# Tuned two-block fp32 kernel on one core: second tiles awaited at use, rotations behind a third tile, one input loaded later, half of the cross output begun inside the attention, roots by exp(-ln/2), squares summed last

## The reference

```python
for i in range(DEPTH):                      # first block, two layers
    u = rms_norm(h, g_mix_norm[i])
    h = h + token_mixers(u, w_in[i], ...)   # two attentions, gates, w_branch_a/b, w_out
    h = h + conv_ffn(rms_norm(h, g_ffn_norm[i]), w_up[i], conv_w[i], conv_b[i], w_down[i])
    ple_gate = jax.nn.sigmoid(rms_norm(h, g_ple_norm[i]) @ w_ple_gate[i])
    h = h + ple_gate * (p[i] @ w_ple_proj[i])
for i in range(DEPTH):                      # second block, two layers
    # mixer of four groups (convolutions, a recurrence, an attention) @ w_out, added to h
    # q = rms_norm(rms_norm(h) @ x_wq, x_qn), k likewise of mem; o = attention(q, k, v) @ x_wo, added
    # h = h + (silu(n @ w1) * (n @ w3)) @ w2   with n = rms_norm(h)
```

## Time and profile before

| | |
|---|---|
| three runs | 3471.82, 3479.12, 3483.51 us; median 3479.12 |
| profiled execution, own time | 3473.41 us |
| its span | 3471.6 us |
| TensorE busy | 3182.2 us, 92% of the span |
| VectorE, ScalarE, GpSimd busy | 1679.7 (48%), 1434.4 (41%), 1576.5 us (45%) |
| mean granted TensorE clock | 0.951 |
| HBM read | 260.46 MB, 76 GB/s over the span |

### The profile page before, as it was taken

The page is one execution under the profiler, slowest core; times in us unless marked ns, Lnnn a source line. Parts: engine busy times, 40 slices in busy tenths (PEclk is TensorE's granted clock), DMA queues, the critical chain, the costliest instruction groups (busy, mean ns, idle before and its releaser), DMA issues. The chain is left out here.

```text
span 3471.6 us, 39165 instructions
## 1 busy us (share of the span) xinstructions
PE 3182.2 (92%) x14620; PEld 2475.1 (71%) x14620; DVE 1679.7 (48%) x2524; ACT 1434.4 (41%) x2281; POOL 1576.5 (45%) x870
## 2 busy tenths in 40 slices
PE   7978999999998799999999968899999985979999
PEld 6655688878776567887878736578877862758887
DVE  2673347731358533775245884433313785443320
ACT  4826533333384564333343444432223354352221
POOL 4623545544564355554555332344445432234443
PEclk8989999999899999999999978999999997889999
DMA  3211233333221122333322101123333200213333
GB/s 113 61 55 42 68 93 97 97 97 103 76 61 61 35 62 93 98 97 95 108 82 90 50 12 44 61 85 97 98 96 98 68 25 20 72 48 98 96 98 103
DMA packets 73740, 265.09 MB, mean 76 GB/s; under 512 B 8656, under 2 KB 9168, under 8 KB 73168
## 3 DMA queue, kind: packets, MB, share of 16 engines
q1 hardware_dynamic: 73552, 262.59, 24.6%
HBM read 260.46 MB, written 2.10 MB: 76 GB/s over the span
## 5 line engine op out<-in xcount | busy, mean ns | idle before, releaser
L365 POOL TENSOR_TENSOR low<-raw,high 128x1024 fp32r<-128x1024 f32 x482 | 1171.1, 2432 | 1289.2 <-ACT high L356 1269.3
L380 PE MATMUL bank<-slot_r,low 128*128 128x512 f32 (+2 forms) x3636 | 1434.5, 395 | 0.0
L381 PE MATMUL bank<-slot_r,high 128*128 128x512 f32 (+2 forms) x3636 | 1431.9, 394 | 0.0
L379 PE MATMUL bank<-slot_r,high 128*128 128x512 f32 (+1 forms) x3316 | 1337.6, 403 | 75.0 <-POOL low L365 30.8
L356 ACT ACTIVATE high<-raw 128x1024 fp32r<-128x1024 f32 x482 | 506.7, 1054 | 821.3 <-PE bank L381 761.0
L379 PEld LDWEIGHTS bank<-slot_r,high 128*128 128x128 f32 x3316 | 635.0, 192 | 260.1 <-issue 69.6
L380 PEld LDWEIGHTS bank<-slot_r,low 128*128 128x128 f32 (+1 forms) x3636 | 696.6, 192 | 149.0 <-issue 9.4
L381 PEld LDWEIGHTS bank<-slot_r,high 128*128 128x128 f32 (+1 forms) x3636 | 695.5, 191 | 149.4
L1583 DVE SCALAR_TENSOR_TENSOR tmp<-padded,small,tmp 128x512 f32<-128x512 f32 x176 | 210.0, 1251 | 0.0
L840 POOL TENSOR_SCALAR tmp<-tmp,stat 128x512 f32<-128x512 f32 (+3 forms) x128 | 71.5, 559 | 193.0 <-DVE stat L815 169.2
L509 ACT ACTIVATE slot_r<-slots,small 128x512 fp32r<-128x512 f32 (+1 forms) x80 | 54.7, 683 | 207.8 <-DVE slots L1591 73.4
(11 more groups left out here) (310 smaller groups left out, 3584.1 us busy)
## 6 DMA issues: line engine op xcount, KB each, us to landing
raw<-w SPq DMA_DIRECT2D x482, 512.0 KB, 3.6
slots<-x_in SPq DMA_DIRECT2D x4, 512.0 KB, 6.6
slots<-mem_in SPq DMA_DIRECT2D x2, 1024.0 KB, 5.0
out<-slots SPq DMA_DIRECT2D x8, 256.0 KB, 4.8
const<-const_in SPq DMA_DIRECT2D x1, 1073.5 KB, 10.8
padded<-p_in SPq DMA_DIRECT2D x2, 512.0 KB, 5.5
tmp<-masks_in SPq DMA_DIRECT2D x1, 512.0 KB, 11.5
small<-small SPq DMA_DIRECT2D x2, 231.5 KB, 2.7
```

Source lines behind the costliest of these rows:

```text
L365: pool.tensor_tensor(self.low[:, t % PARTS, :], self.raw[:, t % RING, :], self.high[:, t % PARTS, :].bitcast(F32), ALU.subtract).then_inc( ...
L379: pe.matmul(acc, lhs[0], rhs[1], start=first, stop=False)
L380: pe.matmul(acc, lhs[1], rhs[0], start=False, stop=False)
L381: return pe.matmul(acc, lhs[0], rhs[0], start=False, stop=last)
```

## The change

What it does, part by part. In `lead_tiles`, at w_out and the mix of `first_tail`, and at w_out and the query tiles of `second_tail`, the second of two tiles is awaited when its first product comes, not together with the first. In `first_project` the first two rotations stand behind the third tile. The transfer of `p` stands two weight tiles later. The second half of w_ple_proj waits for each bank by itself. In `second_tail` the roots are exp(-ln/2) on ScalarE and the three reciprocals are gone; the second value tile is split ahead of the query's roots; the first x_wo tile is split inside the attention and its four products with the first half of XO stand ahead of the last values; `hf` has seven buffers for squares, its low parts stand one step later, its adds behind all of them, and its total behind the second up tile.

```diff
@@ Prep @@
-        if c >= 3:
-            act.wait_ge(self.sig("added"), c - 2)
-        out = self.squares[c % 2] if c else self.acc
+        if c > len(self.squares):
+            act.wait_ge(self.sig("added"), c - len(self.squares))
+        out = self.squares[c % len(self.squares)] if c else self.acc
@@ lead_tiles; the same edit at mix and w_out of first_tail, at w_out and query of second_tail @@
-        two = [weights.next(pe) for _ in range(2)]
+        two = []
         for ks in (range(KC - 1), range(KC - 1, KC)):
-            for j, w in enumerate(two):
+            for j in range(2):
+                if len(two) == j:
+                    two.append(weights.next(pe))
+                w = two[j]
@@ first_project @@
-                    if j >= 1:
-                        rotate(j - 1)
+                    for n in ((), (), (0, 1))[j] if j < 3 else (j - 1,):
+                        rotate(n)
@@ first_tail @@
-                weights.load(sp, ffn + 2 * FC + 6)
+                weights.load(sp, ffn + 2 * FC + 8)
                 sp.wait_ge(sem("conv"), 6 * FC)
                 sp.dma_start(padded_t[:, 0:2, 0:SEQ], p_in[layer]).then_inc(sem("load_p"), 16)
...
-                    if half:
-                        pe.wait_ge(sem("ple_product"), 4)
                     w = weights.next(pe)
                     for c in range(4):
+                        if half:
+                            pe.wait_ge(sem("ple_product"), c + 1)
@@ second_tail @@
-        hf = Prep(sem, "hf", xs, [s2("g_ffn", c) for c in range(KC)], u_all, tmp[:, 4, :], [tmp[:, 5, :], tmp[:, 2, :]])
+        hf = Prep(sem, "hf", xs, [s2("g_ffn", c) for c in range(KC)], u_all, tmp[:, 4, :], [tmp[:, i, :] for i in (5, 2, 0, 1, 3, 8, 9)])
+        def side_pe(pe, step, place):
+            if step == 4 * NT + 4 and place == "turns":
+                out_tile.append(weights.next(pe))
+                pe.wait_ge(sem("o_low"), 1)
+                for n in range(4):
+                    product(pe, banks[n][:, :], part(out_tile[0], slice(None), slice(2 * n * P, 2 * n * P + P)), pair(XO_HIGH, XO_LOW), True, False)
+
+        def side_act(act, step):
+            if step == 2 * NT + 6:
+                act.wait_ge(sem("out_ready"), 2)
+                act.activation(R[XO_HIGH][:, :], S[:, XO, :], ACT.Copy).then_inc(sem("o_high"), 1)
+                weights.split_high(act, o_at + 1)
+
+        def side_dve(dve, step, place):
+            if step == 4 * NT and place == "end":
+                dve.wait_ge(sem("o_high"), 1)
+                dve.tensor_tensor(R[XO_LOW][:, :], S[:, XO, :], R[XO_HIGH][:, :].bitcast(F32), ALU.subtract).then_inc(sem("o_low"), 1)
+
+        def side_pool(pool, n):
+            if n == 2 * NT + 4:
+                weights.split_low(pool, o_at + 1)
...
-                    if s == 0:
+                    if s == 1:
                         hf.total(pe, banks[6][:, :], cst("ones"))
...
-                        act.activation(K_R, K_R, ACT.Sqrt, scale=1.0 / 64).then_inc(sem("key_root"), 1)
+                        act.activation(K_R, K_R, ACT.Ln, scale=1.0 / 64).then_inc(sem("key_log"), 1)
+                        act.wait_ge(sem("key_log"), 1)
+                        act.activation(K_R, K_R, ACT.Exp, scale=-0.5).then_inc(sem("key_rstd"), 1)
...
+                weights.split_high(act, q_at + 4)
                 for c in range(2):
                     act.wait_ge(sem("query_biased"), c + 1)
-                    act.activation(tmp[:, 2 + c, :], tmp[:, 2 + c, :], ACT.Sqrt, scale=1.0 / 64).then_inc(sem("query_root"), 1)
+                    act.activation(tmp[:, 2 + c, :], tmp[:, 2 + c, :], ACT.Ln, scale=1.0 / 64).then_inc(sem("query_log"), 1)
+                for c in range(2):
+                    act.wait_ge(sem("query_log"), c + 1)
+                    act.activation(tmp[:, 2 + c, :], tmp[:, 2 + c, :], ACT.Exp, scale=-0.5).then_inc(sem("query_rstd"), 1)
                 weights.split_high(act, q_at + 5)
...
-                        dve.wait_ge(sem("key_root"), 1)
-                        dve.reciprocal(K_R, K_R).then_inc(sem("key_rstd"), 1)
...
-                    dve.wait_ge(sem("query_root"), c + 1)
-                    dve.reciprocal(r, r).then_inc(sem("query_rstd"), 1)
...
                     dve.tensor_tensor(S[:, X + c, :], S[:, X + c, :], banks[c][:, :], ALU.add).then_inc(sem("x_crossed"), 1)
-                    hf.low(dve, c)
                     if c >= 1:
-                        hf.add(dve, c)
+                        hf.low(dve, c - 1)
+                hf.low(dve, KC - 1)
+                for c in range(1, KC):
+                    hf.add(dve, c)
```

More of the change, by code:

```diff
@@ L525, in add @@
             eng.wait_ge(self.sig("added"), c - 1)
-        eng.tensor_tensor(self.acc, self.acc, self.squares[c % 2], ALU.add).then_inc(self.sig("added"), 1)
+        eng.tensor_tensor(self.acc, self.acc, self.squares[c % len(self.squares)], ALU.add).then_inc(self.sig("added"), 1)
     def total(self, pe, bank, ones, carried=False):
@@ L1420, in _ @@
                 mixed = [pair(MIX_HIGH + k, MIX_LOW[k]) for k in range(KC)]
-                two = [weights.next(pe) for _ in range(2)]
+                two = []
                 for ks in (range(KC - 1), range(KC - 1, KC)):
-                    for c, w in enumerate(two):
+                    for c in range(2):
+                        if len(two) == c:
+                            two.append(weights.next(pe))
+                        w = two[c]
                         for k in ks:
@@ L2435, in _ @@
                 for half in range(2):
-                    w = weights.next(pe)
+                    w = out_tile[0] if half == 0 else weights.next(pe)
                     for n in range(4):
                         c = 4 * half + n
-                        for k in range(2):
+                        for k in range(1 - half, 2):
                             if c == 0:
-                                pe.wait_ge(sem("o_low"), k + 1)
+                                pe.wait_ge(sem("o_low"), 2)
                             mm = product(pe, banks[c][:, :], part(w, slice(None), slice((2 * n + k) * P, (2 * n + k + 1) * P)),
```

14 lines of the change are left out of this document (7 added, 7 removed).

## The result

| | before | after |
|---|---|---|
| median | 3478.72 us (four runs) | 3425.52 us (3422.87 to 3426.14, four runs) |
| ratio | | 0.9853, 95% interval 0.9841 to 0.9865 |
| span of the profiled execution | 3471.6 us | 3423.2 us |
| TensorE busy | 3182.2 us | 3168.6 us |
| mean granted clock of that execution | 0.951 | 0.955 |

The change saves 53 us by the medians, 48.4 by the two profiled spans. Forecast were 61 and a range that holds the result. The difference of the spans splits into 13.6 us that TensorE was busy less (3182.2 - 3168.6: the same 14620 matmuls, less of them at the lower clock) and 34.8 that it stood less. One timed run of a later kernel (roots alone: 3704.31 us, mean clock 0.824, against 3463.06 to 3469.08 for its five others) was in a slower state and is left out of its median and ratio.

A forecast was written before the change was run, and what follows sets the result against it. TensorE, busy 3182.2 of 3471.6 us, was taken as the bound, so only its waits and half-clock work could be won. Terms summed to 60.7: 3473.4 becomes 3412.7, plus 5.7 for the median gives 3418; range 3403 to 3446.

The forecast's parts named there:

- start, w_out, w_ple_proj, leads, query pair: Waits for second tiles and banks go: 2.8 at the start, 13.6 at w_out, 4.3, 2.8, and 1.42 per query pair.
- rotations: First projection, both layers: the third tile goes first, so the narrow tile begins 4.8 and 5.3 us sooner; 10 us.
- roots (with the query pair's 2.8): Query roots by log and exponential bring ScalarE to the attention sooner: 6.1 us a layer, 12.2 in all.
- cross output and hf: From x_wo to the fourth up tile: 7.75 us a layer, 15 in all, called the softest term; bounds 0 and 10 a layer.
- the drain: About 1.38 us added to each table load by the Trainium skill's rule; would cost 2.8 in all, time 3421.
- p at no cost: Moving the transfer of p two tiles later costs 0; without cover, up to 2.5 us a layer.
- the new waits of 2.7 and 2.6: Expected waits: about 2.8 us at x_wo's second half and a new one of about 2.4 at the fourth up tile.
- Rival B: Second-tile waits are only passed on a tile: about 47 us saved, 3432; A or B alone had 0.21.
- D: Slower: the clock is granted late more often, 150 us more at the lower level, 3493; chance 0.02.
- E: Nothing changes: all the waits are passed on to the end of a block, 3479; chance 0.03.
- C: More saved: upper clock throughout narrow tile and x_wo, no wait in the fourth up tile; 73 us, 3406; chance 0.05.
- A: Last terms passed on: 4 of the 15 and 9 of the 12.2 left, 3433; A or B alone had 0.21.

The follow-up runs named there:

- two_tiles: Kernel before with only the second of two tiles awaited at its first product, and w_ple_proj's second-half banks one by one: 3449.56 us, ratio 0.9923.
- hf_only: Kernel before with only the hf part: seven square buffers, later low parts, adds behind them, total behind the second up tile: 3467.01 us, ratio 0.9968.
- port: Changed kernel with GpSimd held ahead of the third up tile's low part until the seven adds are done: 3424.92 us, ratio 0.9841 to before.
- the last kernel: Changed kernel with two w_down tiles split ahead, the fourth up tile ahead, values copied before the first x_wo high part: 3392.52 us, ratio 0.9763.

## Why the prediction was right, and where it was off

The forecast of 3418 missed the median by 7.5 us, 14% of the saving. Its terms, each against what the parts gave alone (ratio times 3478) and in the ledger:

| part | forecast | alone | in the ledger |
|---|---|---|---|
| start, w_out, w_ple_proj, leads, query pair | 26 | 27 | 28 |
| rotations | 10 | 8 | 9 to 12 |
| roots (with the query pair's 2.8) | 12 | 10 | 13, less 3.6 in the attention |
| cross output and hf | 15 | 0 + 11 | 9 (11 in the second profile) |

The parts alone sum to 27 + 8 + 10.4 + 11.1 + 0.3 = 57. About 2 of it are counted twice: from the first sum at w_out of `second_tail` to the first scores it is 63.16 and 63.14 before in the two layers, 56.95 in both with the roots alone and 56.6 with everything, while the second tiles alone save 0.9 and 1.7, so that they add only 0.4 a layer to the roots. That leaves 55 against 51 by the ratio and 53 by the medians: as far as intervals of 3 to 7 us to either side of a part can say, the change is additive.

**Confirmed:** the idle times at w_out with the slow stretch behind each (7.3 and 6.8 in the ledger, 7.0 and 6.6 forecast), and that nothing is passed on; the rotations' 4.8; the root's chain, 6.6 at the first scores (forecast 6.1), without the drain; p at no cost (no wait appears at w_down or w_ple_proj); the new waits of 2.7 and 2.6; the fall of the waits for low parts to 36.4 (about 35). The clock is at the edge of what was asked, 0.955 or more: 0.955 in the profiled execution, but 0.953 to 0.954 in the three other timed runs and 0.953 in the second profile. Rival B is refuted by two_tiles, D and E by the time, C by the wait in the fourth up tile. Of A a part is true: the cross output and `hf` lose 4 to 6 of their 15, where it has 11, and the roots 2 of their 12, where it has 3.

**Off:** the step "Cross output and `hf`". It had two faults. The first is attribution: I let the first half's 12 products shorten the way to the first up tile, when the eight chunks' chain through VectorE sets that, as the 2.74 us a chunk, which I used myself, already said. Moved early it makes the chain begin later: without it the root comes 1.8 sooner (42.04). The half alone gives 0.0 (0.9999), so all of the gain is hf's. The second is a size: I counted the seven adds at 0.69 each, 4.8 us. They take 7.47, since GpSimd's low part of the third up tile falls in them, and without it 5.46. Up to the adds the chain came as forecast (32.6 behind the first values for the first up tile's end, the first add at 32.5). It did not get there by the 2.74: with the sum's passes gone a chunk takes 1.3, and 3.0 and 3.3 the two times that VectorE's low pass takes 2.48 and 2.38 beside a low part of GpSimd. So VectorE's first scaling by the root came 1.9 us sooner behind the first values than before (43.85 in place of 45.79) and not 3.8. The Trainium skill's page "GPSIMD Engine Reference", section "1. Specifications", says that GpSimd shares its SBUF interfaces with VectorE and contends with instructions of two SBUF inputs; hf_only and port agree, with their 7.47 and 5.46. It gives no size. Had I counted the two as wholly exclusive, an estimate beforehand would have been 4.8 and a low part of 2.4, 7.2. What remained was given back in part in the fourth up tile: its wait of 2.58 was forecast, the lower clock behind it (0.3 in one layer and 1.9 in the other, the distances 13.80 and 15.34 less 10.88 and 2.58) was not.

The roots' term was right at the place and came short at the time. The attention's first steps after the wait of 2.80 ran at clock 0.50, in the third layer in both profiles of the changed kernel:

```profile
2183.00:2185.00 2.00, 2.00 (x8) 0.50 0.00 0
...
2187.00:2189.00 2.00, 2.00 (x9) 0.50 0.02 4
2189.00:2191.00 2.00, 2.00 (x10) 0.50 0.01 4
```

That gave back 2.2 and 1.4 in the ledger. The kernel before has the same low clock there in its second profile, so no single pair of profiles can say how much belongs to the change, but all of them together can. From the first scores to the first values it is 10.9 us in eight of the twelve passages of kernels with the old roots, and 12.6 in four. In the sixteen of kernels with the new roots it is 12.2 to 13.2, never less. The means, 11.5 and 12.8, put 1.3 a layer on the new roots, 2.6 in all, and the ledger's 13 less that is about the 10.4 of the roots alone (five runs, interval 6 to 15). The mean granted clock over the 10.9 us from the first scores says the same: 1.00 in the eight, 0.69 in the four, 0.55 to 0.69 in the sixteen. That the longer wait ahead of the scores is the reason, 2.8 (2.0 in the last kernel) in place of 1.1, is argued and not shown.

A third shortfall is in no term: the sum counts the stretches that the change doesn't touch at nothing, and in both pairs of profiles they cost 5 us net, 2.9 and 4.7 lost and 2.4 gained. That the total came within 7.5 us owes something to terms that brought more than forecast (28 in place of 26).

The largest thing to be won lay outside the change: the three waits at w_down, which are among the fourteen of the earlier trace rows, brought 25 us when they went, nearly as much as the largest part of the change (27) and half of all its parts together (53).

## What to carry to other kernels

Before starting work early on one engine, find which chain makes its consumer wait: 12 products moved ahead were worth nothing, since the chain behind them ran through VectorE at 2.74 us a chunk. An in-order engine that waits for something late should have split what its neighbours need first (two high parts ahead of a wait: 25 us). Look in the trace of before for every instruction that the change adds: another place of the kernel may already have it, as the Ln and Exp pair here. Price a wait of the busy engine with the slow clock behind it, here 2.5 us on top of 5.5, and price VectorE's passes over two SBUF inputs with GpSimd's beside them.

## What the hardware showed unexpectedly

At some places the granted clock of the same instructions differs from execution to execution: 1.00 in one profile of the kernel before and 0.50 in the other at 2152 to 2154 and 2224 to 2226, 3.8 us in the span. At others it repeats: a stretch of 334 us came out alike to 0.1 us in two executions of one kernel and 4.7 us longer, at the lower mean clock of 0.87, in both executions of another kernel with the same 1653 matmuls there. So a difference of up to 4 us between single profiles can be chance, and a difference that a second profile of both kernels confirms can still come from a stretch that the edit doesn't touch.

VectorE and GpSimd hold each other up when both read two SBUF inputs: seven adds take 7.47 us beside one low part and 5.46 without it (one add 2.70 in place of 0.69), and the low part 2.89 against 2.36.

A table load between Ln and Exp costs 1.28 us and 0.04 of gaps, in the new roots as in those of the norms before.
